# Row-step pipelines in the attention mixers of a four-layer network, and weight subtractions in pieces of 512 columns

## What is computed

```python
h = layernorm(ALPHA * h + mix(h)); h = layernorm(ALPHA * h + swiglu(h))      # four times
# mix 1 (MLA), 8 heads: c_q, c_kv, k_rope = split(x @ w_in); c_q, c_kv = rmsnorm(...)
logits = (q_nope @ k_nope.T + rope(q_rope) @ rope(k_rope).T) * scale          # 128 and 64 deep
o = softmax(where(chunk_mask, logits, -1e30)) @ v                             # query blocks of 128
# mix 2 (differential), 8 heads of 2 x 64: two softmaxes with a distance bias
a = p[0] - lam * p[1];  o = rmsnorm(a @ v, g_sub) * (1 - lambda_init)
# mix 3 (even): a gated 3-tap convolution and a multiscale pool
# mix 4 (odd): 8 heads of 64 with forget gates on half of the width; on the other half
# GLU -> causal depthwise convolution of 31 taps -> layer norm -> swish
```

## Time and profile before

| | us |
|---|---|
| median of three runs | 2426.18 |
| lowest and highest run | 2425.48, 2428.16 |
| the profiled execution | 2430.45 |
| its span | 2428.7 |
| PE busy (96% of the span) | 2341.0 |
| POOL, DVE, ACT busy | 1056.1, 753.6, 664.3 |

### The profile page before, as it was taken

How to read it: one execution, slowest core, us unless ns; L and a number is a source line. 1 busy time by engine, 2 the same in 40 slices (tenths; PEclk the granted TensorE clock), 3 DMA queues, 4 the chain that set the end, 5 groups by cost and what they waited for, 6 DMA issues and landing times.

```text
span 2428.7 us, 24625 instructions
## 1 busy us (share of the span) xinstructions
PE 2341.0 (96%) x10347; PEld 1867.6 (77%) x10347; DVE 753.6 (31%) x1434; ACT 664.3 (27%) x889; POOL 1056.1 (43%) x369
## 2 busy tenths in 40 slices
PE   8999999999999989999999999999998998999998
PEld 6666788888777668888878878888876666888887
DVE  6565200002555550000046230010169635000003
ACT  2222322222232322212222222222243463221221
POOL 4213454454323336544445645545431224654443
PEclk9999999999999989999999999999999999999999
DMA  5103222222211113222223222222220112322221
GB/s 198 40 35 121 104 88 104 95 88 95 96 53 44 65 57 122 104 94 97 83 91 108 104 105 102 89 104 78 96 95 27 44 53 87 121 104 95 96 83 56
DMA packets 32366, 213.91 MB, mean 88 GB/s; under 512 B 3584, under 2 KB 4736, under 8 KB 9216
## 3 DMA queue, kind: packets, MB, share of 16 engines
q1 hardware_dynamic: 32256, 212.34, 24.5%
HBM read 210.23 MB, written 2.10 MB: 87 GB/s over the span
## 4 chain that ended last, share of the span: by engine, by line
PE 89%; DVE 8%; ACT 1%; issue 1%; POOL 1%; DMA 0%; SPq 0%; DVEq 0%; ACTq 0%
PE bank L891 17%; PE bank L893 17%; PE bank L892 17%; PE bank L941 9%; PE bank L943 9%; PE bank L942 9%; PE bank L922 3%; DVE bank L1872 2%; PE bank L1172 1%; PE bank L927 1%; PE bank L1074 1%; PE bank L1234 1%; PE bank L1153 1%; PE bank L1279 1%; PE bank L1232 1%
## 5 line engine op out<-in xcount | busy, mean ns | idle before, releaser
L738 POOL TENSOR_TENSOR wlo<-raw,whi 128x2048 fp32r<-128x2048 f32 (+4 forms) x184 | 848.9, 4616 | 534.8 <-ACT whi L420 534.8
L891 PE MATMUL bank<-XH,whi 128*128 128x512 f32 x1832 | 722.4, 394 | 7.3 <-POOL wlo L792 6.2
L893 PE MATMUL bank<-XH,wlo 128*128 128x512 f32 x1832 | 714.9, 390 | 0.0
L892 PE MATMUL bank<-XL,whi 128*128 128x512 f32 x1832 | 714.7, 390 | 0.0
L420 ACT CAST whi<-raw 128x2048 fp32r<-128x2048 f32 (+4 forms) x184 | 350.6, 1909 | 410.3 <-PE bank L941 300.6
L891 PEld LDWEIGHTS bank<-XH,whi 128*128 128x128 f32 x1832 | 344.8, 188 | 97.4 <-issue 20.6
L893 PEld LDWEIGHTS bank<-XH,wlo 128*128 128x128 f32 x1832 | 344.7, 188 | 73.0
L892 PEld LDWEIGHTS bank<-XL,whi 128*128 128x128 f32 x1832 | 345.0, 188 | 69.6
L1571 DVE TENSOR_TENSOR hf<-sil,bank 128x512 f32<-128x512 f32 x88 | 60.5, 687 | 902.4 <-PE bank L893 855.1
L752 POOL TENSOR_TENSOR HL<-hf,HH 128x512 fp32r<-128x512 f32 x88 | 113.9, 1295 | 399.4 <-ACT HH L458 399.4
L941 PE MATMUL bank<-whi,HH 128*128 128x512 f32 x704 | 274.4, 390 | 0.0
(11 more groups left out here) (247 smaller groups left out, 2187.2 us busy)
## 6 DMA issues: line engine op xcount, KB each, us to landing
raw<-w_ffn_gu SPq DMA_DIRECT2D x88, 1024.0 KB, 4.7
raw<-w_ffn_dn SPq DMA_DIRECT2D x40, 1024.0 KB, 4.7
raw<-w_diff_in SPq DMA_DIRECT2D x7, 1536.0 KB, 6.5
GB<-gb SPq DMA_DIRECT2D x8, 1024.0 KB, 7.3
raw<-w_ev_in SPq DMA_DIRECT2D x6, 1024.0 KB, 4.8
raw<-w_od_in SPq DMA_DIRECT2D x4, 1536.0 KB, 6.6
raw<-w_mla_pair SPq DMA_DIRECT2D x4, 1280.0 KB, 6.3
raw<-w_mla_o SPq DMA_DIRECT2D x4, 1024.0 KB, 5.8
```

The lines of the kernel that those rows point to most:

```text
L738: pool.tensor_tensor(wlo[:, off:off + size], raw[:, off:off + size], whi[:, off:off + size].bitcast(F32), ALU.subtract).then_inc(lo_ready, 1)
L891: release(pe.matmul(out, whi[:, off:off + P], xh, start=start, stop=False))
L892: pe.matmul(out, whi[:, off:off + P], xl, start=False, stop=False)
L893: return pe.matmul(out, wlo[:, off:off + P], xh, start=False, stop=stop)
```

## The change

Three things change. First, MLA and the differential mixer become pipelines of row steps like the odd mixer. MLA handles both heads of a pair in one step, with the two 128-deep products first and then the two 64-deep ones. ACT scales rows and keeps transposed probabilities. In the differential mixer one DVE pass combines the two unscaled rows (the common factor falls out in the norm, whose epsilon is scaled by the squared sum), ACT makes the distance bias and the high part of each head, and POOL its low part, head by head. Second, the swapped rope columns go: DVE multiplies four groups of 32 partitions by the sine and writes each to its partner's place (`rope`). The order of units and tiles in MLA changes with it: keys, values and their latents first. In the odd mixer, the high and low parts of outputs 0 and 1 are made when they arrive, ACT builds the last diagonals before it keeps the convolution of tile 1, and one weight split moves one step forward. Third, POOL subtracts each weight unit in pieces of 512 columns. The load of the first norm's `GB` moves behind the last MLA output.

```diff
-STREAM = [("mla_in", (3072, 3072, 1024)), ("mla_pair", (2560,) * 4), ("mla_o", OUT), ("ffn0", None),
+STREAM = [("mla_in", (3072, 3072)), ("mla_pair", (2176,) * 4), ("mla_o", OUT), ("ffn0", None),
...
-PLACED = {("mla_o", 1): 2048, ("diff_in0", 1): 1536}
+PLACED = {("ffn0_gu", 1): 0, ("diff_in0", 1): 1536}
...
-DIFF_SLOTS = (STEPS[0:5], STEPS[5:10], STEPS[10:15], STEPS[15:19], STEPS[19:22], STEPS[22:24])
+DIFF_SLOTS = (STEPS[0:4], STEPS[4:6], STEPS[6:10], STEPS[10:12], STEPS[12:16], STEPS[16:18], STEPS[18:24], [])
 ODD_SLOTS = (STEPS[0:4], STEPS[4:6], STEPS[6:10], STEPS[10:12], STEPS[12:16], STEPS[16:18], STEPS[18:21], STEPS[21:24])
 ODD_SETS = ((0, 1, 4, 5), (6, 7, 2, 3))
-MLA_K = (3, 3, 3, 3, 2, 2, 2, 2)
-MLA_SLOTS = tuple([(t, k) for k in range(MLA_K[t])] if t is not None else [] for t in (0, 1, 2, 3, 4, None, 5, 6, 7))
+MLA_K = (2, 2, 2, 2, 3, 3, 3)
+MLA_STEPS = [(t, k) for t in range(7) for k in range(MLA_K[t])]
+MLA_SLOTS = (MLA_STEPS[0:3], MLA_STEPS[3:5], MLA_STEPS[5:8], MLA_STEPS[8:9], MLA_STEPS[9:12], MLA_STEPS[12:13], MLA_STEPS[13:17], [])
...
-                if norm:
-                    sp.wait_ge(xn_ready, 8 * norm)
+                sp.wait_ge(*((xn_ready, 8 * norm) if norm else (va_free, 16)))
                 if norm == 6:
-                    sp.wait_ge(va_free, 8)
+                    sp.wait_ge(va_free, 48)
                 sp.dma_start(GB[:], gb[norm]).then_inc(gb_in, 16)
 
             norms = Count()
             for u in range(2, len(UNITS)):
                 load(u)
-                if u == 9:
-                    sp.wait_ge(w_used, 7)
+                if u == FIRST_UNIT["mla_o"] + 2:
...
+            def mla_high(p):
+                for m in range(2):
+                    vax.add()
+                    act.wait_ge(va_done, vax.at())
+                    act.copy(XH[:, 2 * p + m, :], bank[6 + m][:]).then_inc(oh_ready, 1)
+            for s in range(17):
+                p, qb = divmod(s, 4)
+                if s < 16:
+                    for m in range(2):
+                        c = 2 * (s % 2) + m
+                        exp_row(mL[s % 2][m][:, 0:(qb + 1) * P], negmax[:, c:c + 1], rowsum[:, c:c + 1])
+                    sums_inverted()
+                    for m in range(2):
+                        c = 2 * (s % 2) + m
+                        scale_row(mL[s % 2][m][:, 0:(qb + 1) * P], rinv[:, c:c + 1])
+                if qb == 0 and s < 16:
+                    vax.add(2)
+                if qb == 1 and p:
+                    mla_high(p - 1)
+                for m in range(2) if s else ():
+                    keep_p(mPT[m], 6 + m, (s - 1) % 4)
+                if qb == 1 and p < 3 or s in (12, 13):
+                    split_w()
+                if p < 3 and qb == 3:
+                    tiles.add(7)
+            mla_high(3)
...
+            def high_head(h):
+                vax.add()
+                act.wait_ge(va_free, vax.at())
+                act.copy(YH[:, h, :], dO[h % 2][:]).then_inc(act_hi, 1)
+            distances(0)
+            for s in range(33):
+                h, j = divmod(s, 4)
+                if s < 32:
+                    n, c = (j + 1) * P, 2 * (s % 2)
                     for m in range(2):
+                        exp_row(dL[s % 2][m][:, 0:n], negmax[:, c + m:c + m + 1], rowsum[:, c + m:c + m + 1])
+                    if j == 0 or j == 1 and h:
+                        vax.add()
+                if s:
+                    keep_p(dPT, 6, (s - 1) % 4)
+                if j == 2 and h < 7:
+                    distances(h + 1)
+                if j == 3 and h:
+                    high_head(h - 1)
+                if j == 0 and h < 7 or s in (28, 30):
+                    split_w()
...
+            diagonals(range(20, TAPS))
             keep_conv(1, conv_done, 1)
-            diagonals(range(20, TAPS))
...
-                if s == 12:
...
-                    for k in (0, 1):
-                        act.copy(XH[:, k, :], fY[:, k, :]).then_inc(act_hi, 1)
...
-                    pool.tensor_tensor(wlo[:, off:off + size], raw[:, off:off + size],
-                                       whi[:, off:off + size].bitcast(F32), ALU.subtract).then_inc(lo_ready, 1)
+                    for a in range(off, off + size, HALF):
+                        part = slice(a, min(a + HALF, off + size))
+                        ins = pool.tensor_tensor(wlo[:, part], raw[:, part], whi[:, part].bitcast(F32), ALU.subtract)
+                    ins.then_inc(lo_ready, 1)
...
+            for h in range(9):
+                if h < 8:
+                    split_w()
+                if h:
                     inverse_root()
-                if j in (4, 5):
+                    split_x(YL[:, h - 1, :], dO[(h - 1) % 2][:], YH[:, h - 1, :])
+                if h == 7:
                     split_w()
...
+            off = begin_unit()
+            pe.wait_ge(latent_lo, 2)
+            mla_steps(off, MLA_STEPS[0:5])
+            mean_squares(5, sq[1], QR)
+            mla_steps(off, MLA_STEPS[5:8])
             spread_root(6)
+            for k in range(3):
+                pe.wait_ge(latent_lo, 3 + k)
+                mla_steps(off, MLA_STEPS[8 + k:9 + k])
+            mla_steps(off, MLA_STEPS[11:])
+            out_ready = {}
...
+            def mla_attend(p):
+                for m in range(2):
+                    pe.wait_ge(tr_free, trs.at(m - 1))
+                    claim(6 + m)
+                    value_end(attend(6 + m, slice(0, P), mV[p % 2][m], slice(0, P), mPT[m]), 6 + m)
+                    out_ready[2 * p + m] = (va_free, vas.n)
+            def mla_out(k):
+                out_k(off, k % 4, *attended(k), out_ready[k], k == 0, k == KD - 1)
+            for s in range(16):
+                p, qb = divmod(s, 4)
+                i, n = p % 2, (qb + 1) * P
+                if qb == 0:
+                    pe.wait_ge(tile_free, tiles.at())
+                    pe.wait_ge(rope_ready, p + 2)
+                    off = begin_unit()
+                if s == 14:
+                    off = begin_unit()
+                for m in range(2):
+                    claim(4 + m)
+                    pe.matmul(bank[4 + m][:, 0:n], mQN[i][m][:, qb * P:n], mKN[i][m][:, 0:n], start=True, stop=False)
+                for m in range(2):
                     half = slice(64 * m, 64 * m + 64)
+                    logit_end(pe.matmul(bank[4 + m][:, 0:n], mQR[i][half, qb * P:n], KR[half, 0:n], start=False, stop=True), 4 + m)
+                if qb == 0:
+                    for m in range(2):
+                        v_transposes(6 + m, mVT[m], tiles.at())
+                if qb == 1 and p:
+                    mla_attend(p - 1)
                 if p < 3:
+                    mla_steps(off, MLA_SLOTS[2 * qb])
                 else:
+                    mla_out((0, 2, 4, 5)[qb])
+                for m in range(2) if s else ():
+                    p_transposes(6 + m, mL[(s - 1) % 2][m], (s - 1) % 4 + 1)
                 if p < 3:
+                    mla_steps(off, MLA_SLOTS[2 * qb + 1])
+                elif qb < 2:
+                    mla_out((1, 3)[qb])
+            for m in range(2):
+                p_transposes(6 + m, mL[1][m], NB)
+            mla_attend(3)
+            def mla_late():
+                mla_out(6)
+                mla_out(7)
+            out_pair(OUT_KS, attended, (mla_late,))
...
+            for s in range(32):
+                h, j = divmod(s, 4)
+                i, n = h % 2, (j + 1) * P
+                if j == 0:
+                    pe.wait_ge(tile_free, tiles.at())
+                    off = begin_unit()
+                if s == 30:
+                    off = begin_unit()
+                claim(4)
+                claim(5)
+                for m in range(2):
+                    half = slice(64 * m, 64 * m + 64)
+                    logit_end(pe.matmul(bank[4 + m][:, 0:n], dQ[i][half, j * P:n], dK[i][half, 0:n], start=True, stop=True), 4 + m)
+                if j == 0:
+                    v_transposes(7, dVT, tiles.at())
+                if h and j == 1:
+                    diff_attend(h - 1)
+                if h < 7:
+                    head_steps(off, DIFF_SLOTS[2 * j])
+                else:
+                    diff_out((0, 2, 4, 5)[j])
+                if h and j == 2:
+                    squares_of_head()
+                if h and j == 3:
+                    spread_of_head()
+                if s:
+                    p_transposes(6, dL[(s - 1) % 2][0], (s - 1) % 4 + 1)
+                if h < 7:
+                    head_steps(off, DIFF_SLOTS[2 * j + 1])
+                elif j < 2:
+                    diff_out((1, 3)[j])
+            p_transposes(6, dL[1][0], NB)
+            diff_out(6)
+            diff_attend(7)
+            out_pair(OUT_KS, headed, (squares_of_head, spread_of_head, lambda: diff_out(7)))
...
+            def rope(dst, b):
+                dve.wait_ge(tile_done, tiles.at(1))
+                for q in range(4):
```

(62 more changed lines are left out.)

453 lines of the change are left out of this document (133 added, 320 removed).

## The result

| | us |
|---|---|
| before, median of four runs (lowest, highest) | 2426.11 (2425.48, 2428.16) |
| after, median of four runs (lowest, highest) | 2386.10 (2384.65, 2386.72) |
| ratio, 95% interval | 0.9833, 0.9816 to 0.985 |
| the profiled execution of after, its span | 2385.82, 2384.0 |

The change makes the kernel 40.0 us (1.7%) faster; 52 were forecast. The time lies inside the range, and inside the forecast's own range of 2362 to 2388, near its upper end. What follows is about the 12 us that are missing, and about two terms of MLA that came out right for reasons that were in part wrong.

A forecast was written before the change was run, and what follows sets the result against it. TensorE was taken as the bound, busy nearly always, with some 80 us of waits plus slow clock. Terms of -32.0 MLA, -14.6 differential, -1 even and norm, -7.3 odd, +3.2 clock gave -51.7: median 2374 us, range 2353 to 2398.

The forecast's parts named there:

- Start: MLA's start: +1.7 us beside its matmuls (-2 to +6); first logits at about 65.5, 7.5 us earlier; PE waits about 5 us.
- MLA, matmuls and rope products: MLA: 60 matmuls removed, -13.6 us; 64-row rope products of two heads side by side, -11.7 us (bounds 0 to 11.7).
- Rival (C): MLA: rope products don't overlap, as both accumulate into banks just written; +11.7 us, 2386; chance 0.07.
- MLA, waits: MLA: PE's 4.7 us on mL and a 3.2 us slow stretch go, -7.9 us; new waits +1.
- "About 0": GpSimd's pieces outside the differential mixer's end: no net gain, but -1 us for even mixer and norm together.
- The offset of the profiled execution: Whole kernel: the profiled execution lay 4.3 us above the median; the same difference was taken off the new sum.
- Differential mixer, heads: Seven heads: -0.6 us; row stalls go, 6.6 with pipeline restart; new dK waits 5.1, first head's logits +0.9.
- Differential mixer, its end: Last head and end: -14 us; 19.1 of waits and slow clock go, +5.1 new for low parts and last unit.
- Odd mixer: Before attention -4 us, DVE's chain of taps being the bound; attention -3.3 us (-9.4 gone, +6.1 new waits).
- (A): Whole kernel: new waits replace old; only 25.3 us of PE work and 4 before odd attention go: 2397; chance 0.15.
- (B): Start, differential and odd mixers: three quarters of new waits and slow clock are covered, 18 us less, 2356; chance 0.14.
- (D): Feed-forward stages: POOL becomes the bound; at 2.7 us a piece +54 us, 2480, slower; chance 0.03.

## Why the prediction was right, and where it was not

**Start.** The new side is right: first logits at 64.97, forecast about 65.5, and PE's wait 4.7 us, forecast about 5. The old side was misread. At 73.05 PE had issued the last of the first pair's value transposes; the first logits started behind them and a wait on the values:

```profile
74.16 0.46 PE L1232 MATMUL bank<-mKN,mQN 128*128 128x128 f32 x2 [0.88 <-DVE mV L1634]
```

And the first pair has 8 records of value transposes, not 16; they stood ahead of the old logits and stand behind the new ones. Past logits and transposes PE goes on with weights at 66.88 instead of 74.96, 8.1 us earlier. The sum has 5.8 (7.5 for the matmuls, less 1.7), so this term was short by 2.3.

**MLA, matmuls and rope products.** Right. By the counts 62 records fewer in the two stretches, 60 expected (a few records can be missing); the four rope records take 1.06 us, and undoing their pairing costs 13.6 us by the stage, where 11.7 + 1.8 was expected. Rival (C) falls.

**MLA, waits.** What the sum takes off went, but the reason was incomplete. I laid the waits on mL and the stretch at 156.7 to rows wanted too early. The run with pieces alone shows that a hold of DVE by POOL, the 4.38 us row at 150.60, stood behind much of them: 6.4 us in that pair of profiles, though only 1.8 in the medians. I had read this very mechanism from a row of the odd mixer (1812.20) and looked for it there and in the even mixer only. The changed kernel's MLA is safe from it twice, since ScalarE now scales the rows, and since POOL works in pieces; taking the pieces away from it changed nothing there (218.06 us up to the first feed-forward product, against 218.37). "About 0" for the pieces is right for the changed kernel as a whole, and wrong as a statement on the pieces by themselves in MLA. The stage gave 4.9 us more than the sum has: 2.3 at the start, and 0.4 because the transposes that end it ran mostly at full clock (before, a slow stretch began at 252.2); the last 2.2 I can't assign.

**The offset of the profiled execution.** Wrong. The profile of before lay 4.3 us above its median, and I took the same off the new sum. The profile of after lies at its own median (2385.82 and 2386.10). The excess of before goes with the clock: its mean granted clock was 0.983, and 41 executions of it, run beside the later kernels, have 0.984 to 0.987, the slower ones the lower. In which stage it lay no run shows; if it was a slow stretch in MLA, as the 6.4 us in a profile against 1.8 us in the medians of the run with pieces alone suggest, then part of what I counted as won is not there in most executions. It accounts for 4 to 5 of the 12 us.

**Differential mixer, heads.** The mechanism was right, two sizes were off. The old stalls for rows, counted at 6.6 us, were 0.97 us at five heads by the spacing of starts, 4.8. And the new wait on dK was forecast at 0.85 us, six times, and measured 1.35, six times, 3.0 us more. I let DVE scale and copy from the moment that PE begins its transposes. The trace has DVE waiting for the spread root 1.60 us more, so that it scales at 680.35, when those transposes are all but done:

```profile
680.35 0.75 DVE L1804 SCALAR_TENSOR_TENSOR dO<-dO,gsub,bank 128x512 f32<-128x512 f32 x1 [1.60 <-PE bank L1295]
681.01 0.68 DVE L1518 COPY dK<-bank 128x512 f32<-128x512 f32 x1
```

```profile
680.08 0.49 PE L984 MATMUL bank<-cons,dL 128*128 128x128 f32 x3
681.75 0.49 PE L1326 MATMUL bank<-dK,dQ 64*128 64x128 f32 x4 [1.18 <-DVE dK L1518]
```

At the first head PE goes on with weights 2.0 us later than before (20.62 against 18.62 us from the stage's start) instead of 0.9. Of this a new slow stretch at 586.1 makes 1.6; the wait on dK is 1.6 us long, but took the place of two of 0.9 together.

**Differential mixer, its end.** This is the term that failed. What I said would go did go. The new low parts and the last unit cost 1.4 and 2.5 us, a little less than the 2.0 and 3.1 counted. What I left out is what is late next: the norm's root, behind a POOL unit whose place in POOL's order the change doesn't touch. PE came to the norm's first X with nothing between it and the root, and waited 4.1 us. Two slow stretches begin in this part, at 818.2 and 849.0, where I had counted one in the whole kernel, in a term of its own. The first costs 1.6 us by the spacing of starts. The second costs nothing that can be seen: from the first transposes of X to the last it takes 16.79 us (850.13 to 866.92), and in the kernel before, without a stretch, 16.76 (888.25 to 905.01). I had even written down that POOL subtracts later, and followed that to PE's wlo only. By the stages the mixer missed its forecast by 14.0 us: 3.0 on the copies, 1.8 on the old stalls, 1.1 at the first head, 4.1 on X and 1.6 of clock can be named; the last 2.4 us, net of small gains, I can't assign. Of these the copies are shown by an experiment. The 4.1 us are the length of a wait: each kernel that moved the root had POOL's pieces beside DVE's chain in its place, so none shows the norm without that price.

**Even mixer.** -1 forecast, 142.69 us in both. Nothing.

**Odd mixer.** Right in both parts. Before attention -3.4 us against -4 (106.36 to 102.93), with DVE free of idle time, as said, and PE's 9.0 us moved to the wait on fK, 9.9. In attention -2.9 against -3.3, with the new waits at 2.3, 1.0 and 1.9 us where 2.5, 1.4 and 2.2 stood.

**Rivals.** (A) was near in time (2397) and true in one mixer out of three: there new waits took the place of the old. (B) and (D) fall: the new waits weren't covered, and POOL's 512-column piece took 1.29 us, far from 2.4. The measured time is rival (C)'s 2386 by chance only; the run with the products apart shows that its mechanism isn't there.

## What to carry to other kernels

When a wait on the main engine goes, follow every engine's queue to the next thing that the main engine needs, also into the stage behind the change: here a root of one column stood behind a unit of 2048. In a queue that feeds a tight loop put what is awaited first; one copy moved ahead of one scaling was worth 7 us. A short wait of TensorE can cost more in clock behind it, where TensorE is then the bound, and where the wait can't be removed, throwaway products in a free bank are cheap to try.

## What the runs showed of the hardware

- Eight of nine waits of TensorE, 3.1 to 4.7 us long, had a slow stretch begin at or near them; with products put into the wait no stretch began there, at the norms in two kernels and at the two other places in one. 2.6 us of extra products at each of seven norms gave 9.5 us back. Inside the differential norm, where PE waits for DVE's chain, a stretch of 6.8 us more or less changed the 16.3 to 16.8 us between the first transposes of X and the last by 0.1.
- Two 64-row products of 512 columns on different halves of the array, accumulating into two banks that 128-row products had just written, took 1.06 us together and 1.05 each when apart.
- A DVE scaling of 256 columns took 4.38 us beside a POOL subtraction of 2048 columns, and 1.06 beside pieces of 512. A DVE combination of 256 columns took 5.62 beside a subtraction of 3072, and PE didn't wait for it in the pipeline of row steps. Four DVE operations with two SBUF tensors each, in a row beside four such pieces, took 6.41 us instead of 2.82, so pieces shorten a hold but not the sum of a chain.
- The mean granted clock of a run tells most of its spread: 2363.8 us at 0.997 and 2368.1 us at 0.993 in the same kernel.
